# A later point for three weight splits at the end of each feed-forward stage

## The reference

```
h = rms_norm(x) * (1 + scale0) + shift0
x = x + 0.5 * gate0 * swiglu(h, w13[0], w2[0])      # ("f", l, 0)
h = rms_norm(x) * (1 + scale1) + shift1
x = x + gate1 * token_mixer(h, w_in, ..., w_out)     # ("m", l)
h = rms_norm(x) * (1 + scale2) + shift2
x = x + 0.5 * gate2 * swiglu(h, w13[1], w2[1])       # ("f", l, 1)
```

## Time and profile before

| what | value |
|---|---|
| time, median of 3 | 1537.4 us (1535.63 to 1538.65) |
| the profiled execution | 1538.65 us, with a span of 1536.3 us |
| PE busy | 1503.1 us (98% of the span) |
| DVE busy | 1156.9 us (75%) |
| ACT busy | 792.2 us (52%) |
| mean granted TensorE clock | 0.992 |

### The profile page before, as it was taken

The page is one execution under the profiler, slowest core; times in us unless marked ns, Lnnn a source line. Parts: engine busy times, 40 slices in busy tenths (PEclk is TensorE's granted clock), DMA queues, the critical chain, the costliest instruction groups (busy, mean ns, idle before and its releaser), DMA issues. The chain is left out here.

```text
span 1536.3 us, 21156 instructions
## 1 busy us (share of the span) xinstructions
PE 1503.1 (98%) x8530; PEld 1289.1 (84%) x8530; DVE 1156.9 (75%) x1593; ACT 792.2 (52%) x1124; POOL 24.3 (2%) x31
## 2 busy tenths in 40 slices
PE   8997999999999999999999999999999999999998
PEld 7885988888888888878788888888888787888886
DVE  6796688888877987767677887788877677778654
ACT  7546455444455553466556554455544655465541
POOL 0020000000000000000000000000000000000000
PEclk9998999999999999999999999999999999999999
DMA  8123377777746877633236877677776433366450
GB/s 339 61 104 113 131 277 303 291 279 307 299 165 258 303 271 262 237 139 127 92 137 249 287 273 260 247 271 277 262 269 242 148 110 110 138 235 244 175 195 28
DMA packets 57008, 327.07 MB, mean 213 GB/s; under 512 B 6592, under 2 KB 6976, under 8 KB 27456
## 3 DMA queue, kind: packets, MB, share of 16 engines
q1 hardware_dynamic: 55440, 322.76, 56.9%
q10 hardware_dynamic: 1472, 2.97, 0.5%
HBM read 324.65 MB, written 1.05 MB: 212 GB/s over the span
## 5 line engine op out<-in xcount | busy, mean ns | idle before, releaser
L286 DVE TENSOR_TENSOR wlo<-raw,whi 128x2048 fp32r<-128x2048 f32 (+2 forms) x236 | 533.7, 2265 | 107.4 <-ACT whi L279 106.6
L279 ACT ACTIVATE whi<-raw 128x2048 fp32r<-128x2048 f32 (+2 forms) x236 | 445.7, 1894 | 150.5 <-PE ps L1540 142.0
L1305 PE MATMUL ps<-hreg_r,whi 128*128 128x512 f32 x1760 | 420.2, 391 | 0.8 <-DVE mix L1479 0.5
L1305 PEld LDWEIGHTS ps<-hreg_r,whi 128*128 128x128 f32 x1760 | 324.1, 188 | 64.6 <-issue 0.7
L1314 PEld LDWEIGHTS ps<-hreg_r,wlo 128*128 128x128 f32 x1760 | 225.4, 191 | 8.3
L1314 PE MATMUL ps<-hreg_r,wlo 128*128 128x256 f32 x1760 | 228.8, 283 | 0.0
L1473 ACT ACTIVATE mix<-ps 128x512 f32<-128x512 f32 x109 | 65.2, 598 | 278.3 <-PE ps L1314 278.3
L321 DVE CUSTOM_DVE_ANT_0 adaw<-adaw,crow,colp 128x1024 f32<-128x1024 f32 x144 | 182.3, 1279 | 19.1 <-DMA adaw<-in_wada 19.0
L1532 PE MATMUL ps<-whi,ireg_r 128*128 128x512 f32 x480 | 149.6, 392 | 0.9 <-ACT ireg_r L1433 0.9
L1536 PE MATMUL ps<-wlo,ireg_r 128*128 128x512 f32 x480 | 148.0, 389 | 0.0
L1540 PE MATMUL ps<-whi,ireg_r 128*128 128x512 f32 x480 | 147.9, 389 | 0.0
(11 more groups left out here) (357 smaller groups left out, 1662.7 us busy)
## 6 DMA issues: line engine op xcount, KB each, us to landing
raw<-in_wu SPq DMA_DIRECT2D x230, 1024.0 KB, 5.7
adaw<-in_wada SPq DMA_DIRECT2D x144, 512.0 KB, 4.5
raw<-in_wu SPq DMA_DIRECT2D x4, 568.0 KB, 5.6
raw<-in_wu SPq DMA_DIRECT2D x2, 544.0 KB, 5.3
x<-in_x SPq DMA_DIRECT2D x2, 512.0 KB, 4.4
out<-hreg SPq DMA_DIRECT2D x2, 512.0 KB, 2.7
crow<-in_c ACTq DMA_DIRECT2D x1, 512.0 KB, 8.3
greg<-in_cst ACTq DMA_DIRECT2D x1, 512.0 KB, 14.5
```

Source lines behind the costliest of these rows:

```text
L279: act.activation(self.whi[:, m, 0:width], self.raw[:, n % NRAW, 0:width], ACT.Copy).then_inc(*self.A.done("hi", n))
L286: dve.tensor_tensor(self.wlo[:, m, 0:width], self.raw[:, n % NRAW, 0:width], self.whi[:, m, 0:width].bitcast(F32), ALU.subtract).then_inc( ...
L1305: pe.matmul(self.ps[:, b, :], self.whi[:, m, c:c + 128], self.hboth[:, kt], start=kt == 0, stop=False)
```

## The change

The change touches the end of each feed-forward stage in three places. In ffn_pe (four stages) the pieces of token tile 1 are issued in the order W8 c0, W9 c0, W10 c0, W8 c1, (norm_pe for t = 0), W9 c1, W10 c1; before it was W8 c0, W8 c1, W9 c0, W10 c0, (norm_pe), W9 c1, W10 c1. In ffn_act, only for the two handoffs to a mixer, the split of B0 moves from behind the first square of t = 1 to ahead of turned_act for t = 0, and that of B1 from behind the second square of t = 1 to ahead of it. In ffn_dve, for the same two handoffs, add(1, 0) moves ahead of the lower half of A1. No instruction is added or removed.

```diff
         for j in range(8, 11):
             self.ffn_down_pe(pe, l, i, j, (0,))
-        self.ffn_down_pe(pe, l, i, 8, (1,))
         for c in range(2):
-            for j in (9, 10):
+            for j in range(8, 11):
+                if c == 1 and j == 9 and st != STAGES[-2]:
+                    self.norm_pe(pe, AFTER[st], 0)
                 self.ffn_down_pe(pe, l, i, j, (1,), (c,))
-            if c == 0 and st != STAGES[-2]:
-                self.norm_pe(pe, AFTER[st], 0)
...
         if ns[0] == "m":
             self.ahead_act(act, n + 1)
+            self.ahead_act(act, n + 2)
             self.turned_act(act, ns, 0)
             self.square_act(act, ns, 1, (0,))
-            self.ahead_act(act, n + 2)
+            self.ahead_act(act, n + 3)
             self.square_act(act, ns, 1, (1,))
-            self.ahead_act(act, n + 3)
             self.turned_act(act, ns, 1)
             return
...
         if ns[0] == "m":
+            add(1, 0)
             self.ahead_dve(dve, n + 1)
-            add(1, 0)
             self.turned_dve(dve, ns, 0)
             add(1, 1)
             self.ahead_dve(dve, n + 2)
```

## The result

The changed kernel is slower, by 0.6 to 0.8%. In the first comparison its median was 1545.93 us (8 runs, 1543.76 to 1556.85) against 1538.24 us (8 runs, 1535.63 to 1541.96), a ratio of 1.0075 with a 95% interval of [1.0051, 1.0097]. Two repetitions gave 1.0063 [1.0043, 1.0083] and 1.0068 [1.0044, 1.0091]. Over all runs of the three, the mean is 1549.8 us for the 44 executions of the changed kernel whose clock was recorded (27, 9 and 8) and 1539.0 us for 79 of the kernel before: 10.8 us more. The forecast was 8.0 us more (1545.4 us, 1542.0 to 1549.5). The way was right, and the median of the first 8 runs was near it by luck: the 27 executions on record from that comparison, these 8 among them, have a median of 1550.8 us, past the upper end of the range. About 2.5 us of the difference are missing from the forecast, and most of this document is about them.

The account below looks back on a forecast made before the run. The prediction took PE, busy for 98% of the span, to bound the kernel. Two handoffs to a mixer (5.3 us) and one between the layers (2.7) add 8.0 us to the median of 1537.4: 1545.4 us, range 1542.0 to 1549.5.

Parts of the forecast that it names:

- PE loses nothing by its order alone, the signal of W8 comes 2.72 us later: Around the norm of t = 0: four pieces stay ahead, two behind; unit W8 ends two pieces, 2.72 us, later.
- B0's split before the tiles is the costly step: Handoffs to a mixer: ACT's split waits for W9, tiles 4.1 us late, PE idles 2.3 us; 2.65 us per handoff.
- add(1, 0) costs nothing: Handoffs to a mixer, on DVE: the earlier add takes 1.4 us while DVE would wait for ACT, so 0.
- Between the layers 2.72 us: Handoff between the layers: b0's split waits for the later W8, so the norm of t = 1 moves by 2.72 us.
- Order binds: Handoffs to a mixer: ACT does not go past its waiting split; the whole sum of 8.0 us hangs on it.
- rival 4: Handoffs to a mixer: no stall, ACT serves its ready tiles ahead of the waiting B0 split; 1537.0 us, chance 0.04.
- Rivals 2 and 3: 2: PE's order free between the layers, 1542.7 us, chance 0.08; 3: mixers return the stalls, 1537.4 to 1540.4 us, 0.07.
- the term for the clock: PE's clock after the three handoff gaps: loss bounded by 0 and 5.1 us, taken as 0.
- rival 1: After the handoff gaps the clock falls; one to three falls give 1547.1 to 1550.5 us, chance 0.18.
- A sign that the prediction named: Whole kernel, profile after: PE's busy time unchanged near 1503 us and its idle time up by 8.

Follow-up runs that it names:

- b0_back: Changed kernel with ACT's split of B0 again behind the first square of t = 1 in handoffs to a mixer; ratio to the kernel before 1.0049, mean 1545.8 us.
- pe_only: Kernel before with only PE's new order of pieces, ACT and DVE as before; ratio to the kernel before 1.0050, mean 1547.8 us.
- after_third: Third set of runs of the changed kernel itself, nothing altered; ratio to the kernel before 1.0068.
- fill: Changed kernel with 8 or 6 extra matmuls in PE's handoff gaps, run three times; ratios to the kernel before 1.0067, 1.0074, 1.0057, mean 1549.6 us.
- after_again: Second set of runs of the changed kernel itself, nothing altered, for a second profile; ratio to the kernel before 1.0063.
- busy_delay: Kernel before with 12 or 13 extra matmuls per handoff, making PE late without waiting; ratios to the kernel before 1.0063, 1.0051, 1.0054, mean 1547.8 us.

## Why the prediction was off

- *PE loses nothing by its order alone, the signal of W8 comes 2.72 us later:* right. A1's split starts 0.26 us after the norm's first matmul, where it started 2.47 us ahead of it: 2.73 us.
- *B0's split before the tiles is the costly step:* right, with its sizes. Wait about 2 us: 2.01. Gap 2.3 us: 2.28. Handoff 2.65 us longer: 2.65, in both. b0_back shows that without this step 1.1 us remain.
- *add(1, 0) costs nothing:* it runs in DVE's wait for ACT; between it and A1's lower half DVE still idled 1.19 us in the changed kernel and in b0_back. It even saves time there, as pe_only against b0_back shows (12.67 for 11.52 us); it was not tried by itself.
- *Between the layers 2.72 us:* 2.72 (12.30 or 12.31 for 9.58, in after_third and in the three profiles of fill), 3.31 with a fall in it. In after_again it is 11.90, but the norm of t = 0 came 0.4 us late there, as in pe_only. The gap before line 1331 was 1.65 us for 1.7, that before line 389 0.74 us for about 1 (after_third).
- *Order binds (rival 4):* the tiles' input was there as early as before, and ACT did nothing for 2.01 us ahead of B0's split instead of taking them. The strictly first in, first out queues of the Trainium skill (TensorE: Matmul & The Clock Gate, Architectural detail) agree with the trace for ACT too.
- *Rivals 2 and 3:* the handoff between the layers was not free, and the mixers gave nothing back.
- **The step that failed is the term for the clock.** The prediction took it as 0, "because a part of it would lie under the wait for the diagonal that follows anyway", and let the range take in "all but the last of rival 1's falls". Rival 1 was right that falls follow the gaps. Each of the seven in the handoffs lasted 3.4 us, which is 1.7 us of dense work, its price; of that, 1.4 us showed in a handoff to a mixer and 0.6 us between the layers, so little lay under the wait. But I priced the clock as something that happens or not within a handoff. It is a sum over the whole kernel that varies from execution to execution, in the kernel before too (23.7 us at the lower level on average), and with the change its mean was 7.4 us higher, 2.5 us of time. A sign that the prediction named says the same: PE's busy time was to stay near 1503 us and its idle time to grow by 8, and they came to 1507.0 us and 6.3 us more.
- *The starting point was low, and that was chance.* The forecast of 1545.4 us is 8.0 on the median of three runs. On the mean of 79, 1539.0 us, the same sum gives 1547.0 us. The mean of the changed kernel, 1549.8 us, is 4.4 us over the forecast: 1.6 from the starting point, 2.5 from the clock and 0.3 from the stalls. With the higher starting point alone the range would have ended at 1551.1 us and held the measured time, with the clock's term just as wrong.
- *What stays open* is by what way the mean moved. That it moved is clear (31.1 ± 1.8 us for 23.7 ± 0.8), and filling the handoffs' gaps, which took the falls out of the handoffs, did not bring it back (31.5 ± 2.0). Only suggested: that a delay without gaps moves it in part (busy_delay 26.8 ± 1.5 us, 1.8 standard errors over the kernel before), and that filling the mixers' waits takes most of it away in the changed kernel (24.7 ± 1.4, with a repetition that did not settle it) and nothing in the kernel before. This speaks for the mixers' thin stretches, met at another moment, over the gaps in the handoffs, but no profile shows the mechanism.

## What to carry to other kernels

Before a weight split (or any prefetch) is moved ahead of critical work on an in-order engine, look up which signal it waits for and where the producing engine issues that: here the signal stood behind the very norm whose result the engine was to serve next. Reordering a producer's pieces keeps its own time and still moves every "unit done" signal, and the one that comes later may gate a queue elsewhere. And where a dense kernel's clock falls by chance, keep the mean clock of each run beside its time and compare at equal clock: so the 8.3 us of stalls were told from the 2.5 us of clock, and the distances from norm to norm agree. Three runs are too few to start a forecast from when single executions of one kernel lie 11 us apart.

## What the runs showed of the hardware

That the changed kernel spends between about 9 us (clock 0.997) and 53 us (0.983) at the lower TensorE clock from one execution to the next, with times from 1542.04 to 1557.35 us over 44 runs, was not expected from three runs of the kernel before within 3 us; that kernel too runs from 1533.3 to 1544.2 us in 79 runs. PE's waits of 1.7 to 2.3 us in the handoffs were followed by a fall in some executions and not in others: in 7 of 18 handoffs, each time for 3.4 us.
